# One layer of a hybrid decoder: gate and value columns loaded in two mixed blocks, all convolution taps on VectorE, attention three units deep and from the widest tile down

## The reference, cut to what matters

```python
q, k, v, bval, bgate = jnp.split(proj, [A_WIDTH, 2*A_WIDTH, 3*A_WIDTH, 3*A_WIDTH + B_WIDTH], axis=-1)
# attention: 8 heads x 64, partial rotary on q and k, causal, three (window, dilation) branches
s = where(valid, (q @ k.T) * dh ** -0.5, NEG_INF); m = max(s); e = exp(s - m); out = (e / sum(e)) @ v
# convolution: gated value, causal depthwise conv of 31 taps, LayerNorm over channels, swish
a = bval * sigmoid(bgate)
y = depthwise_conv(a, conv_w, width=31) + conv_b
b_out = silu(layer_norm(y) * ln_g + ln_b)
h = x + concatenate([a_out, b_out]) @ w_out
```

## Time and profile before

| what | us |
|---|---|
| median of three runs | 2133.05 |
| profiled execution, span from first to last instruction | 2125.8 |
| outside the span, against the median | 7.3 |
| TensorE busy | 1903.9 |
| VectorE busy | 1489.6 |
| ScalarE busy | 1081.2 |
| GpSimd busy | 555.6 |

### The profile page before, as it was taken

The page is one execution under the profiler, slowest core; times in us unless marked ns, Lnnn a source line. Parts: engine busy times, 40 slices in busy tenths (PEclk is TensorE's granted clock), DMA queues, the critical chain, the costliest instruction groups (busy, mean ns, idle before and its releaser), DMA issues.

```text
span 2125.8 us, 22982 instructions
## 1 busy us (share of the span) xinstructions
PE 1903.9 (90%) x8384; PEld 1399.8 (66%) x8384; DVE 1489.6 (70%) x1370; ACT 1081.2 (51%) x1044; POOL 555.6 (26%) x329
## 2 busy tenths in 40 slices
PE   6985888799999999995899999987799999999993
PEld 5763466577766777774777777765577767777762
DVE  3699335498888888885534434346588988888885
ACT  4213243377767777773222222223477777777763
POOL 0589000024433333341000000000033444344330
PEclk9995669799999999997899999998799999999996
DMA  6221003399999999995522222223399999999993
GB/s 241 80 80 40 1 10 129 115 362 357 354 350 359 360 358 355 367 364 211 197 79 80 80 80 79 80 79 114 147 366 360 371 348 360 361 361 358 365 345 145
DMA packets 74601, 491.25 MB, mean 231 GB/s; under 512 B 14896, under 2 KB 23088, under 8 KB 49840
## 3 DMA queue, kind: packets, MB, share of 16 engines
q1 hardware_dynamic: 54832, 455.10, 56.5%
q0 software_dynamic: 14336, 16.82, 2.4%
q10 hardware_dynamic: 5376, 18.57, 2.4%
HBM read 492.53 MB, written 31.46 MB: 246 GB/s over the span
## 4 chain that ended last, share of the span: by engine, by line
PE 34%; DMA 30%; POOL 12%; DVE 11%; issue 8%; ACT 3%; POOLq 1%; ACTq 0%; DVEq 0%; SPq 0%
DMA y_dram<-y_e,scatter_at 27%; PE psum L722 7%; PE psum L724 7%; PE psum L723 7%; POOL scatter_at L1784 5%; POOL x_e L1777 4%; DVE xs L1372 4%; POOL gather_at L1774 2%; PE psum L1052 2%; PE psum L781 2%; PE psum L782 1%; PE psum L786 1%; DMA x_e<-xs_dram,gather_at 1%; ACT w_hi L597 1%; DVE w_lo L616 1%
## 5 line engine op out<-in xcount | busy, mean ns | idle before, releaser
L616 DVE TENSOR_TENSOR w_lo<-raw,w_hi 128x2048 fp32r<-128x2048 f32 x384 | 862.6, 2289 | 127.9 <-ACT w_hi L624 122.7
L624 ACT ACTIVATE w_hi<-raw 128x2048 fp32r<-128x2048 f32 x384 | 712.7, 1910 | 0.0
L781 PE MATMUL psum<-w_hi,uT_hi 128*96 128x512 f32 x1024 | 407.5, 398 | 9.7 <-ACT w_hi L624 5.7
L782 PE MATMUL psum<-w_hi,uT_lo 128*96 128x512 f32 x1024 | 404.2, 395 | 0.0
L1774 POOL COPY gather_at<-index 96x1 uint32 (+1 forms) x64 | 48.8, 762 | 1226.2 <-DVE index L1546 673.6
L603 DVE TENSOR_TENSOR w_lo<-raw,w_hi 128x2048 fp32r<-128x2048 f32 x46 | 106.4, 2314 | 293.6 <-ACT w_hi L597 293.6
L597 ACT ACTIVATE w_hi<-raw 128x2048 fp32r<-128x2048 f32 x46 | 87.8, 1914 | 413.3 <-PE psum L724 411.8
L786 PE MATMUL psum<-w_lo,uT_hi 128*96 128x512 f32 x1024 | 278.7, 394 | 0.0
L781 PEld LDWEIGHTS psum<-w_hi,uT_hi 128*96 128x96 f32 x1024 | 168.9, 165 | 76.6 <-DVE uT_lo L1553 10.6
L786 PEld LDWEIGHTS psum<-w_lo,uT_hi 128*96 128x96 f32 x1024 | 166.4, 163 | 70.8 <-DVE w_lo L616 0.5
L782 PEld LDWEIGHTS psum<-w_hi,uT_lo 128*96 128x96 f32 x1024 | 166.9, 163 | 66.6
(11 more groups left out here) (173 smaller groups left out, 2575.8 us busy)
## 6 DMA issues: line engine op xcount, KB each, us to landing
raw<-in_expert_w_gate SPq DMA_DIRECT2D x64, 2048.0 KB
raw<-in_expert_w_up SPq DMA_DIRECT2D x64, 2048.0 KB
raw<-in_expert_w_down SPq DMA_DIRECT2D x64, 2048.0 KB
raw<-in_odd_w_in SPq DMA_DIRECT2D x8, 2048.0 KB
raw<-in_even_w_in SPq DMA_DIRECT2D x5, 2048.0 KB
raw<-in_odd_w_in SPq DMA_DIRECT2D x8, 1024.0 KB
raw<-in_odd_w_out SPq DMA_DIRECT2D x4, 2048.0 KB
raw<-in_even_w_out SPq DMA_DIRECT2D x2, 2048.0 KB
```

The source lines that it names most:

```text
L616: nc.vector.tensor_tensor(part(w_lo[b]), src, part(w_hi[b]).bitcast(F32), ALU.subtract).then_inc(m.lo[b], 1)
L624: nc.scalar.activation(part(w_hi[b]), src, ACT.Copy).then_inc(m.hi[b], 1)
L781: nc.tensor.matmul(psum[0:r, bank], xeT_hi[:, c, 0:r], hi[:, j], start=(half + j == 0), stop=False)
L782: nc.tensor.matmul(psum[0:r, bank], xeT_lo[:, c, 0:r], hi[:, j], start=False, stop=False)
```

## The change

The taps of all four chunks go to VectorE, in pairs of chunks: 62 taps of chunks 0 and 1, then 62 of chunks 2 and 3. For that the gate and value columns are loaded as two mixed blocks of 256 gate and 256 value columns each, two DMAs a block. GpSimd keeps only the cosines. 88 taps stand among the splits and the rotations, 36 in the first nine attention units, four in each. The attention runs from tile 3 down to tile 0; transposes lag two units and the v product three. Scale, bias and row maximum are one `tensor_tensor_reduce` with the accumulator; the bias table is scaled by 8 for it and the exponential takes scale -1. On ScalarE the copy of unit n - 2 now stands before the exponential of unit n. The denominators have columns of their own for each tile. The channel mean moves to n = 12, the variance to 15. The concatenation is turned about (convolution in chunks 0 to 3, attention in 4 to 7), and TensorE waits for the last turned attention tile only ahead of a block's second half.

```diff
-CONV_AT = 21
+CONV_AT = 12
+TAP_UNITS = 9
+TURN_LAG, VALUE_LAG = 2, 3
+TURN_HEAD = 6
-    return [(q, h) for q in range(TILES) for h in range(A_HEADS)]
+    return [(q, h) for q in reversed(range(TILES)) for h in range(A_HEADS)]
-    even = [("w_in", c) for c in (4, 3, 0, 1, 2)] + [("w_out", c) for c in range(2)]
+    even = [("w_in", c) for c in ("pair0", "pair1", 0, 1, 2)] + [("w_out", c) for c in range(2)]
 # SyncE
+                elif n < 2:
+                    value, gate_at = 3 * A_WIDTH + n * 256, 3 * A_WIDTH + B_WIDTH + n * 256
+                    fill(n, [(blocked(n)[:, :, 0:256], w_in[:, :, gate_at:gate_at + 256]),
+                             (blocked(n)[:, :, 256:], w_in[:, :, value:value + 256])])
 # TensorE
-            for n in range(len(units) + 2):
+            for n in range(len(units) + VALUE_LAG):
...
-                    pe.wait_ge(tap, 3 * TAPS)
-                    pe.wait_ge(tap_pool, TAPS)
+                    pe.wait_ge(tap, BC * TAPS)
...
-            a_transpose(TILES - 1)
-            copied(pe, "aT", TILES - 1)
+            a_transpose(0)
             pe.wait_ge(b_ok, BC)
             for half in range(2):
                 for k in range(2):
+                    if k:
+                        copied(pe, "aT", 0)
                     dense_half(n, k, [("out0", half, q) for q in range(TILES)], cat_hi, cat_lo, False)
 # ScalarE
-            split_hi(act, 1)
-            for c in range(BC): ... Sigmoid
-            split_hi(act, 2)
+            split_hi(act, 1, (0,))
+            gates(0)
+            split_hi(act, 1, (1,))
+            split_hi(act, 2, (0,))
+            gates(2)
+            split_hi(act, 2, (1,))
...
+                m = n - TURN_LAG
+                if 0 <= m < len(units):
+                    src, free = bank("PT", (q, hd))
+                    if m >= 2:
+                        act.wait_ge(pv_done, m - 1)
+                    nc.scalar.activation(probT[:, m % 2, 0:w], src[:, 0:w], ACT.Copy).then_inc(free, 1)
                 if n < len(units):
-                    act.wait_ge(mx_ok, n + 1)
+                    copied(act, "S", (q, hd))
                     nc.scalar.activation(prob[:, n % 2, 0:w], sm[:, n % 2, 0:w], ACT.Exp, bias=stat[:, 16 + n % 2:17 + n % 2],
+                                         scale=-1.0, accum_out=stat[:, total:total + 1]).then_inc(p_ok, 1)
...
-                if n == CONV_AT + 6:
+                if n == CONV_AT + 7:
 # VectorE
+            def gated(first):
+                for c in (first, first + 1): ...
+            def taps(first, last):
                 for i in range(first, last):
-                    k, c = i // 3, i % 3
+                    c = 2 * (i // (2 * TAPS)) + i % 2
+                    k = i % (2 * TAPS) // 2
                     if k:
-                        dve.wait_ge(tap, i - 2)
+                        dve.wait_ge(tap, i - 1)
+            gated(0)
+            split_lo(dve, 1, 1)
             taps(0, 12)
+            split_lo(dve, 2, 0)
+            taps(12, 24)
+            split_lo(dve, 2, 1)
+            gated(2)
+            taps(24, 34)
             split_lo(dve, 3, 0)
-            taps(12, 24)
+            taps(34, 46)
             split_lo(dve, 3, 1)
-            taps(24, 42)
+            taps(46, 58)
             split_lo(dve, 4, 0)
-            taps(42, 51)
+            taps(58, 70)
+            rotate("q")
             split_lo(dve, 4, 1)
-            rotate("q")
+            taps(70, 80)
+            rotate("k")
+            taps(80, 88)
             split_lo(dve, 5, 0)
-            rotate("k")
             split_lo(dve, 5, 1)
...
-                    V.scalar_tensor_tensor(out=sm[:, n % 2, 0:w], in0=src[:, 0:w], scalar=A_DIM ** -0.5,
-                                           in1=bias_a[:, SEQ - w:SEQ], op0=ALU.mult, op1=ALU.add).then_inc(free, 1)
-                    copied(dve, "S", (q, hd))
-                    V.tensor_reduce(stat[:, 16 + n % 2:17 + n % 2], sm[:, n % 2, 0:w], AX.X, ALU.max, negate=True) \
-                        .then_inc(mx_ok, 1)
-                if n < CONV_AT - 1:
-                    taps(min(51 + 3 * n, 3 * TAPS), min(51 + 3 * n + 3, 3 * TAPS))
+                    V.tensor_tensor_reduce(out=sm[:, n % 2, 0:w], in0=src[:, 0:w], in1=bias_a[:, SEQ - w:SEQ],
+                                           scale=-A_DIM ** -0.5, scalar=3e38, op0=ALU.add, op1=ALU.min,
+                                           accum_out=stat[:, 16 + n % 2:17 + n % 2]).then_inc(free, 1)
+                if n < TAP_UNITS:
+                    taps(88 + 4 * n, 88 + 4 * n + 4)
...
-                if n == CONV_AT + 8:
+                if n == CONV_AT + 9:
 # GpSimd
-            copied(pool, "val", BC - 1)
-            taps(0, 9)
             cosines("q")
             cosines("k")
-            taps(9, TAPS)
```

More of the change, by code:

```diff
@@ L91, in shape_constants @@
         count = sum(((dist >= 0) & (dist % dil == 0) & (dist <= win)).astype(np.int64) for win, dil in BRANCHES)
-        bias[:, b * P:(b + 1) * P] = np.where(count > 0, np.log(np.maximum(count, 1)), NEG)
+        bias[:, b * P:(b + 1) * P] = A_DIM ** 0.5 * np.where(count > 0, np.log(np.maximum(count, 1)), NEG)
     tab_a = np.stack([cos_a, sin_a, bias], 1)
@@ L142, in plan_banks @@
     norm(0)
-    for c in range(BC):
-        b.plan(("gate", c))
-    for c in range(BC):
-        b.plan(("val", c))
+    for pair in range(2):
+        for kind in ("gate", "val"):
+            for c in (2 * pair, 2 * pair + 1):
+                b.plan((kind, c))
     for which, c in ROPE_CHUNKS[:4]:
@@ L255, in trunk_kernel @@
     for n in range(moe_start[1] + n_moe):
-        two = first_odd <= n < moe_start[1] and odd_blocks[n - first_odd][0] == "qk"
+        two = first_odd <= n < moe_start[1] and odd_blocks[n - first_odd][0] == "qk" or n in (0, 1) or \
+            n < moe_start[0] and even_blocks[n][0] == "w_out"
         fills[n % SLOTS] += 32 if two else 16
@@ L420, in trunk_kernel @@
         b_ok = sem("b_ok")
-        mx_ok = sem("mx_ok")
         p_ok = sem("p_ok")
@@ L1111, in _, with gates @@
                 norm_copies(0, half)
-            split_hi(act, 1)
-            for c in range(BC):
-                src, free = bank("gate", c)
-                nc.scalar.activation(sigT[:, c], src, ACT.Sigmoid).then_inc(free, 1)
-            split_hi(act, 2)
+            def gates(first):
+                for c in (first, first + 1):
+                    src, free = bank("gate", c)
+                    nc.scalar.activation(sigT[:, c], src, ACT.Sigmoid).then_inc(free, 1)
+            split_hi(act, 1, (0,))
[4 more added lines that the diff above has]
+            split_hi(act, 2, (1,))
             split_hi(act, 3)
```

149 lines of the change are left out of this document (64 added, 85 removed).

## The result

| | us | runs |
|---|---|---|
| before, same chip | 2132.91 (2130.19 to 2142.47) | 4 |
| after | 2081.36 (2074.74 to 2088.82) | 4 |
| ratio | 0.976, 95% interval 0.973 to 0.9791 | |
| after again, another chip (before there 2130.82) | 2085.47 (2077.59 to 2095.4), ratio 0.978, 0.9742 to 0.9819 | 6 |

The kernel is 51.6 us faster on the first chip and 45.4 us on the second; 43.6 were predicted. The predicted 2089.5 us lies 8.1 us above the first median. What follows goes by two milestones inside the profiled span: **T**, the first fused score instruction (or scaling) on VectorE, and **F**, the first product of the output projection. What lies behind F is "the rest".

The account below looks back on a forecast made before the run. VectorE's tap stream was taken as the bound. Projection 14, attention 28 and tail 1.6 us saved, with 0.6 us added for the DMA, gave -43.6 us: median 2133.05 to about 2089.5 us, range 2073 to 2108.

Parts of the forecast that it names:

- The two prices of a tap: VectorE's taps: 737 to 740 ns with GpSimd idle, 1764 to 1801 ns beside its cosines; median 740 ns after.
- Rival C: Taps keep 1.12 us even without GpSimd; output projection starts near 298 us, time 2126 us; chance 0.06.
- Contention in the projection: Input projection: GpSimd's eight cosines hold up VectorE's taps; 7 us taken, up to 8.4 in all.
- the list of VectorE's work: VectorE from 52.5 us in the projection: taps, splits, gated products, rotations, contention, waits; 97.6 us, first fused score at 150.
- If the contention is nil it is 18: Projection's saving: 14 us expected, 18 if GpSimd's cosines held up no taps.
- D: VectorE falls behind in the projection by contention and the new instruction costs 1.4 us: 2100 to 2108 us; chance 0.12.
- First block's load: Projection's first block in two DMAs with 1 KB pieces: +0.6 us, bounds -1.5 and +2.
- The wide units: Attention on tile 3: TensorE's 4.65 us at the low clock hides VectorE's 3.4 us of taps and new instruction.
- B: Wide units keep the full clock and go at VectorE's 3.4 us instead of 4.65: 2075 us; chance 0.15.
- The norm: Convolution's norm in attention: mean 6.0 us, variance 6.4, TensorE stalls of 3.3 and 4.9 us; v products end at 259.2.
- The tail: From last v product to output projection: 1.9 us instead of 3.5, copies hidden behind the first half.
- The fixed rest: From the output projection's start to the end as before, 1820.5 us; wrong if it changes by more than 5 us.

Follow-up runs that it names:

- e3: Changed kernel with 30 unneeded pairs of multiply and add put on GpSimd, 9 before the cosines and 21 behind; 2114.40 us, ratio to before 0.9923.
- e5: Changed kernel with unread TensorE products added: 27 in the wait for the first exponential, two ahead of the scores of units 3 to 11; 2071.27 us, ratio 0.9726.
- e9: Changed kernel with 27 unread products at unit 2, two in each later unit, more in norm waits, late taps three a unit over twelve units; 2080.74 us.
- e4: Changed kernel with transposes one unit and the v product two units behind the scores, as before; 2095.24 us, ratio to before 0.9820.
- e1: Changed kernel with scale and bias in one instruction and the row maximum in a second again; 2092.55 us, ratio to before 0.9832.
- e12: e5 with eight more unread products ahead of the score of n = 15, before the variance; 2074.43 us, ratio to before 0.9726.
- e11: Changed kernel with 27 unread TensorE products in the wait for the first exponential and none in the units; 2082.98 us, ratio to before 0.9739.
- e10: Changed kernel with 27 unread products in the first wait, one in units 3 to 11, norm waits filled, late taps over ten units; 2064.55 us, ratio 0.9655.

## Why the prediction was right, and where it was off

**The two prices of a tap.** Right. Free taps cost 742 to 745 ns in the median against 740 predicted. The Trainium skill's "Vector Engine (DVE) Microarchitecture Reference", section 7, would have halved the throughput of this form in any company; the 108 free taps outside the query's cosines contradict it. The Trainium skill's "SBUF — State Buffer", section "Who interferes with whom", has a VectorE instruction with two SBUF inputs and a GpSimd instruction that reads SBUF contend; the trace agrees, with e3's taps of 1.0 to 1.84 us beside 0.74 free. Rival C was out.

**Contention in the projection.** Mis-sized. The prediction charged 7 us for eight cosines; four taps were held up, 4.2 us, and four additions of the rotation, 1.6 us, so 5.8. T came at 149.59 for a predicted 150: the list of VectorE's work ended where it was expected. But "If the contention is nil it is 18" could not have come out. The list's last split needs the half that ScalarE had rounded at 145.13 (143.22 and 1.91), so T cannot lie before some 147.3; by this estimate from the rows the contention cost no more than 2.3 us at T, and the rest of it would have been waiting for TensorE. The halves kept their step; TensorE left the last one at 143.1 for a predicted 141, and its wait for `w_lo` in this stage, of before in the row below, is gone (D out).

```profile
PE psum L722 <- DVE w_lo L603: 8.1, 2, 4.4
```

**First block's load.** +0.6 predicted, +0.60 measured. That it agrees so closely is partly luck, from two rates of another layer and bounds of -1.5 and +2.

**The wide units.** Right: 4.65 us each at a PEclk of 0.50, VectorE at 3.26 (3.4 predicted), the fused instruction 0.68 and 0.08 us (0.8 taken, between 0.68 and 1.4). B's condition did not hold. "TensorE: Matmul & The Clock Gate", Part 1, of the Trainium skill says that sustained matmul activity releases the throttle; here the trace disagrees: a stretch busy for 24.56 of 26 us stayed at 0.50, and e5's, busy for 23.66, was at 1.00.

**The norm.** The mechanism was right and its terms were too dear, by 3.8 us in all up to the last v product (255.4 for 259.2). The mean began 0.6 us sooner than listed (193.33 for 193.9) and took 5.31 us for 6.0. From its end to the start of the variance passed 8.2 us for 9.0. The variance took 5.36 for 6.4, and the two stalls 2.70 and 4.76 for 3.3 and 4.9. The price of the variance had come from the earlier trace rows. Before's variance (6.62) and e9's mean (6.72) had the clock at 0.50 almost to their end (0.55 and 0.54 over the whole); e5's mean at the full clock took 3.70. Here both had 0.69, as the clock rose earlier inside them. Why it rose earlier than in before stays open. The tail was 2.2 us from the last v product (254.87 and 0.53) to F, for 1.9; with it F was 257.62 for 261.1.

**Costed at nothing, and worth something.** The text gave the depth and the fusion no term of their own beside the wide units. e4 and e1 show 9.0 and 4.3 us. Both had been weighed where TensorE's 4.65 us hide everything. The depth acts behind the variance, where the clock is up and a unit takes 1.4 to 1.9 us; of the fusion's 4.3 us, 1.5 lie in the first units, which go at VectorE's pace, and 2.7 in the norm. In the sum they were contained, since the list was laid out with them; the explanation of it was not.

**What each part is worth.** Undone one at a time: GpSimd's share 27.9 (put back as work of no use), mixed blocks 16.7, wide tiles first 15.9, depth 9.0, fusion 4.3 us; together 73.8 for a gain of 47.65. And done alone, moving the taps brings 8.7. The parts lean on one another: room on VectorE is worth most where the order puts the taps under long units.

**Around the span.** The prediction laid 7.3 us around before's span by setting it against the median. After's profiled execution has a time of its own, 2074.74 for a span of 2072.9: only 1.84 us lie around it, the other 5 were scatter of that execution. As it entered both sides alike, it cancelled in the difference. The sum put the 0.6 us of the load on top of 261.1, so its forecast of F is 261.7, and F came 4.1 us sooner. Of the 8.1 us by which the median of after was lower than predicted, 4.1 are F; the remainder lies in the rest, within its scatter, and on the second chip the whole miss is 4.0.

**The fixed rest.** Expected within 5 us of 1820.5; 1815.3 and 1834.8. The first is just outside, the second far, and by the prediction's own sign ("changes by more than 5 us") it was wrong on this point. The assumption "same code, same time" held as a mean (1822.1 over the 14 executions) and not for one execution: they lie from 1804.6 to 1834.8, eight of them more than 5 us from 1820.5. The bound had been set without a second trace of before.

## What to carry to other kernels

Where VectorE and GpSimd both read SBUF, price the second engine's help by what it takes from the first: 60 GpSimd instructions in e3 lengthened VectorE's taps by 34.8 us. Giving one engine's work to the other was worth 28 us here with an order that lays the long stream under the longest units of TensorE and starts it as early as its input allows, and 8.7 us in the old order. Judge a local change by a milestone inside the span if a later stage scatters by more than the effect. Look for what a pipeline's depth buys in its quick stretches, not in those where one engine hides everything.

## What the runs showed of the hardware

A long stretch of small products without gaps ran at 1.2 GHz (0.50 in 24.56 busy of 26 us); with 27 products of 128x512 in the wait ahead of it and two more in each unit, the same stretch ran at 2.4 GHz and a unit was 30% shorter (3.27 against 4.65 us in e5; the same in e12, 3.00 with three taps a unit in e9). With the 27 alone (e11), or the 27 and one in each unit (e10), it was back at 1.2 GHz within the first units. The fused instruction costs no more than the plain one on the same bytes (0.68 us at 512 wide) and 0.08 us to read its result. Which of the two engines pays depends on which had begun: the four cosines of the query took 6.91 us before, 8.02 in after, where the first began during a split of VectorE and took 2.87, and 10.39 in e3.
